# A gated linear attention layer whose chunk loop is written out: scores of the next chunk before the head sums, no GpSimd copies, output projection in two halves

## The reference, cut to what matters

```python
def gla_chunked(q, k, v, gk):
    # S_t = diag(exp(gk_t)) S_{t-1} + k_t v_t^T ; o_t = q_t S_t, per head
    def step(state, inp):
        qi, ki, vi, gi = inp
        b = jnp.cumsum(gi, axis=2)
        o_inter = jnp.einsum('bhcd,bhde->bhce', qi * jnp.exp(b), state)
        ...
        o_intra = jnp.einsum('bhij,bhje->bhie', att, vi)
        state = state * jnp.exp(b_last)[:, :, 0, :, None] + jnp.einsum('bhcd,bhce->bhde', ki * jnp.exp(b_last - b), vi)
        return state, o_inter + o_intra

def odd_mixer(h, w_in, gate_up, gate_b, onorm, w_out):
    p = h @ w_in                      # q, k, v, gate input gd, output gate og
    gk = jax.nn.log_sigmoid((gd @ gate_up + gate_b).astype(jnp.float32)) / GLA_GATE_NORM
    o = gla_chunked(q, k, v, gk)
    o = rmsnorm(o, onorm).reshape(B, S, VW) * jax.nn.silu(og)
    return o.astype(h.dtype) @ w_out
```

## Time and profile before

| what | value |
|---|---|
| median of 3 runs | 2069.48 us (2065.72 to 2070.42) |
| profiled execution: its own time | 2070.38 us |
| its span, first to last instruction | 2068.6 us |
| mean granted TensorE clock, share of full speed | 0.958 |
| TensorE busy | 1937.5 us, 94% of the span |
| VectorE, ScalarE, GpSimd busy | 620.2, 460.2 and 209.8 us |
| from chunk 0's first value matmul to the output projection's first matmul | 1312.82 to 1358.38 us |
| the output projection to its last residual add's end | 1358.38 to 1416.67 us |

### The profile page before, as it was taken

One profiled execution on the slowest core, in us unless ns is written; L12 is line 12 of the kernel. 1 busy time (PEld: TensorE's weight loads), 2 busy tenths in 40 slices (PEclk: granted clock), 3 DMA queues, 4 the chain that ended last, 5 costly groups with the idle time before them and its releaser, 6 DMA issues.

```text
span 2068.6 us, 22048 instructions
## 1 busy us (share of the span) xinstructions
PE 1937.5 (94%) x8209; PEld 960.4 (46%) x8209; DVE 620.2 (30%) x1029; ACT 460.2 (22%) x791; POOL 209.8 (10%) x238
## 2 busy tenths in 40 slices
PE   7999898999978999999998999989968999999997
PEld 3554888746453333333333443644453333333333
DVE  2153766532241232223123004211241222123223
ACT  3254332132311111111112004511311111111113
POOL 2000444110001000000000000220100000000000
PEclk9999998999968999999999999999968999999999
DMA  6210100025028999999995113104038999999992
GB/s 174 81 41 0 42 1 1 1 85 220 3 103 332 424 423 424 423 423 424 422 424 196 42 42 120 41 0 163 3 122 344 422 423 424 422 424 422 424 423 84
DMA packets 88654, 466.25 MB, mean 225 GB/s; under 512 B 22426, under 2 KB 24586, under 8 KB 47642
## 3 DMA queue, kind: packets, MB, share of 16 engines
q1 hardware_dynamic: 77024, 448.88, 53.5%
q10 hardware_dynamic: 6682, 8.25, 1.2%
q0 software_dynamic: 4896, 8.40, 1.1%
HBM read 468.64 MB, written 6.29 MB: 230 GB/s over the span
## 4 chain that ended last, share of the span: by engine, by line
PE 85%; DMA 6%; DVE 5%; ACT 2%; issue 1%; POOL 1%; SPq 0%; ACTq 0%; DVEq 0%; POOLq 0%
PE ps L987 80%; DMA W<-in_moe_w 5%; PE ps L1540 1%; PE ps L1511 1%; PE ps L1171 1%; DVE XI L1804 1%; DVE HT L1629 1%; DMA xin<-in_x 0%; PE ps L1483 0%; DVE XJ L1800 0%; DMA xg<-hrows,idc 0%; PE ps L1108 0%; ACT L690 0%; PE ps L1372 0%; POOL memN L573 0%
## 5 line engine op out<-in xcount | busy, mean ns | idle before, releaser
L987 PE MATMUL ps<-W,xgT 128*64 128x512 f32 x2048 | 457.4, 599 | 5.8 <-DMA W<-in_moe_w 3.0
L987 PE MATMUL ps<-HT,W 128*128 128x512 f32 (+1 forms) x896 | 405.4, 611 | 18.8 <-DVE HT L1629 10.4
L987 PEld LDWEIGHTS ps<-HT,W 128*128 128x128 f32 (+1 forms) x896 | 172.7, 195 | 239.2 <-issue 226.0
L987 PEld LDWEIGHTS ps<-W,xgT 128*64 128x64 f32 x2048 | 144.5, 138 | 289.8 <-issue 278.3
L2027 DVE TENSOR_TENSOR XT<-ps,XT 128x512 f32<-128x512 f32 x240 | 166.0, 692 | 236.9 <-PE ps L987 236.9
L987 PE MATMUL ps<-W,act 128*64 128x512 f32 x1024 | 232.3, 595 | 2.8 <-ACT ysb L950 2.8
L987 PE MATMUL ps<-spread,ysb 128*128 128x512 f32 x512 | 228.3, 599 | 3.2 <-ACT ysb L950 3.2
L2019 DVE TENSOR_TENSOR act<-ps,sl 128x256 f32<-128x256 f32 x64 | 26.9, 420 | 450.6 <-ACT sl L945 450.6
L987 PEld LDWEIGHTS ps<-spread,ysb 128*128 128x128 f32 x512 | 94.6, 190 | 136.5 <-issue 136.5
L941 ACT ACTIVATE hs<-ps 128x512 f32<-128x512 f32 x64 | 38.2, 597 | 438.9 <-PE ps L987 438.9
L987 PEld LDWEIGHTS ps<-W,act 128*64 128x64 f32 x1024 | 70.8, 137 | 136.4 <-issue 136.4
(11 more groups left out here) (361 smaller groups left out, 1781.6 us busy)
## 6 DMA issues: line engine op xcount, KB each, us to landing
W<-in_moe_w SPq DMA_DIRECT2D x256, 1024.0 KB, 17.0
W<-in_moe_w SPq DMA_DIRECT2D x64, 2048.0 KB, 16.2
W<-in_od_w_in SPq DMA_DIRECT2D x6, 2048.0 KB, 8.1
W<-in_ev_w_in SPq DMA_DIRECT2D x3, 2048.0 KB, 7.8
W<-in_xa_wq SPq DMA_DIRECT2D x2, 2048.0 KB, 8.6
W<-in_xa_wo SPq DMA_DIRECT2D x2, 2048.0 KB, 10.4
hrows<-hk ACTq DMA_DIRECT2D x8, 512.0 KB, 2.7
W<-in_od_w_out SPq DMA_DIRECT2D x2, 2048.0 KB, 7.8
```

The lines of the kernel that those rows point to most:

```text
L987: return te.matmul(o, l, r, start=first, stop=last)
```

## The change

The loops over the four chunks become straight code on TensorE, VectorE and ScalarE. Within it:
- GpSimd's copies and the tiles `gkc` and `gvc` are gone; TensorE reads `gk` and `gv` in place.
- A function `open_chunk(c)` holds the 4 transposes (bank 7) and the 4 score matmuls (bank 6) of a chunk. That of chunk 0 stands before the last gate projection; that of chunk c+1 stands behind chunk c's state matmuls and before its head sums. The last chunk has no transposes and no state matmuls.
- The head sums go to bank 0 and wait only for the squares. The copy of y out of banks 2 and 3 is waited for before the next chunk's values.
- ScalarE copies the turned keys of the next chunk after its copy of y and before the Ln. VectorE masks chunk 0 before the last gate multiply, and later chunks after the state's two operations. GpSimd's second multiply waits for all eight `og` tiles by a semaphore of its own, `og_in`.
- The output projection goes in two halves of 256 tokens, each 8 tiles of 8 matmuls with 256 columns. The first (banks 2 and 3, columns 0 to 255) waits for two chunks of `g_out` and for the last copy of y; the second (banks 0 and 1, columns 256 to 511) for all of `g_out`. VectorE adds both, in 16 adds.

The core of the diff:

```diff
@@ GpSimd, odd() @@
-                copy(0)
-                copy(1)
                 for c in range(NCH):
...
+                    pool.wait_ge(s["og_in"], KD)
                     g.tensor_tensor(y, y, og[:, :, c * CH:c * CH + CH], ALU.mult).then_inc(s["g_out"], 1)
-                    if c + 2 < NCH:
-                        copy(c + 2)
@@ ScalarE, odd() @@
+                def take_keys(c):
+                    act.wait_ge(s["g_turned"], c + 1)
+                    sc.activation(gkt[:, :], ps[:, 7, :], ACT.Copy).then_inc(s["g_tok"], 1)
+
                 for j in range(KD):
                     take(og[:, j, :], func=ACT.Silu)
+                    if j == KD - 2:
+                        take_keys(0)
...
-                with act.Fori(0, NCH) as c:
-                    act.wait_ge(s["g_turned"], c + 1)
-                    sc.activation(gkt[:, :], ps[:, 0, :], ACT.Copy).then_inc(s["g_tok"], 1)
+                for c in range(NCH):
                     act.wait_ge(s["g_y"], c + 1)
...
+                    if c + 2 < NCH:
+                        take_keys(c + 1)
                     act.wait_ge(s["g_sum"], c + 1)
-                    act.wait_ge(s["g_out"], c + 1)
-                    inverse_root(grs[:, :, :].rearrange("p h t -> p (h t)"), ps[:, 6, :], 256, 0, s["g_ln"], c + 1).then_inc(s["g_rs"], 1)
+                    if c:
+                        act.wait_ge(s["g_half"], c)
+                    inverse_root(grs[:, :, :].rearrange("p h t -> p (h t)"), ps[:, 0, :], 256, 0, s["g_ln"], c + 1).then_inc(s["g_rs"], 1)
@@ TensorE, odd() @@
+                def open_chunk(c):
+                    t = slice(c * CH, c * CH + CH)
+                    if c + 1 < NCH:
+                        for h in range(4):
+                            ins = te.transpose(ps[:, 7, h * P:h * P + P], gk[:, h, t], ident[:, :])
+                        ins.then_inc(s["g_turned"], 1)
+                    for h in range(4):
+                        ins = mm(ps[:, 6, h * P:h * P + P], gk[:, h, t], gq[:, h, t])
+                    ins.then_inc(s["g_mat"], 1)
+
                 for name in ("od_og0", "od_og1"):
                     slot = weights(name)
                     for j in range(4):
+                        if name == "od_og1" and j == 3:
+                            pe.wait_ge(s["g_scaled"], 1)
+                            open_chunk(0)
                         project(bank(), [(W8[slot][:, k, P * j:P * j + P], HT[:, k, :]) for k in range(KD)])
                 pe.wait_ge(s["proj_taken"], n["proj"])
...
+                for c in range(NCH):
+                    t = slice(c * CH, c * CH + CH)
+                    pe.wait_ge(s["g_masked"], c + 1)
+                    pe.wait_ge(s["g_state"], c + 1)
+                    if c:
+                        pe.wait_ge(s["g_sq"], 2 * c)
+                    for e in range(KD):
+                        o = ps[:, 2 + e // 4, P * (e % 4):P * (e % 4) + P]
+                        mm(o, gv[:, c, e * P:e * P + P], gat[:, e // 2, :], True, False)
+                        ins = mm(o, gsn[:, e // 2, P * (e % 2):P * (e % 2) + P], gq[:, e // 2, t], False, True)
+                    ins.then_inc(s["g_y"], 1)
+                    if c + 1 < NCH:
                         pe.wait_ge(s["g_tok"], c + 1)
                         for h in range(4):
-                            ins = mm(ps[:, 4 + h // 2, 256 * (h % 2):256 * (h % 2) + 256], gkt[:, h * P:h * P + P], gvc[b][:, 256 * h:256 * h + 256])
+                            ins = mm(ps[:, 4 + h // 2, 256 * (h % 2):256 * (h % 2) + 256], gkt[:, h * P:h * P + P], gv[:, c, 256 * h:256 * h + 256])
                         ins.then_inc(s["g_added"], 1)
-                        pe.wait_ge(s["g_sq"], c * 2 + 2)
...
+                        open_chunk(c + 1)
+                    pe.wait_ge(s["g_sq"], 2 * c + 1)
+                    for h in range(4):
+                        for u in range(2):
+                            ins = mm(ps[:, 0, h * P:h * P + P], ones[:, :], gsq[:, 2 * h + u, :], u == 0, u == 1)
+                    ins.then_inc(s["g_sum"], 1)
...
+                pe.wait_ge(s["g_out"], NCH // 2)
+                pe.wait_ge(s["g_sq"], 2 * NCH)
+                for mt in range(KD):
+                    if mt >= 2:
+                        pe.wait_ge(s["half_in"], KD + mt - 1)
+                    for k, (l, r) in enumerate(tiles(slice(0, SEQ // 2))(mt)):
+                        ins = mm(ps[:, 2 + mt % 2, 0:SEQ // 2], l, r, k == 0, k == KD - 1)
+                    ins.then_inc(s["half_done"], 1)
+                pe.wait_ge(s["g_out"], NCH)
+                pe.wait_ge(s["g_tok"], NCH - 1)
+                residual(tiles(slice(SEQ // 2, SEQ)), KD, at=0, cols=slice(SEQ // 2, SEQ))
@@ VectorE, odd() @@
-                with dve.Fori(0, NCH) as c:
+                for c in range(NCH):
+                    if c:
+                        mask(c)
+                    if c + 1 < NCH:
+                        dve.wait_ge(s["g_added"], c + 1)
+                        st.then(ve.tensor_tensor(gsn[:, :, :], ps[:, 4:6, :].rearrange("p b (h v) -> p (b h) v", h=2), gsn[:, :, :], ALU.add))
+                        ve.tensor_tensor(gsn[:, :, :], gsn[:, :, :], bcast(gnext[:, :, c:c + 1], [P, 4, 256]), ALU.mult).then_inc(s["g_state"], 1)
+                for mt in range(KD):
+                    dve.wait_ge(s["half_done"], KD + mt + 1)
+                    cols = slice(0, SEQ // 2)
+                    ve.tensor_tensor(XT[:, mt, cols], ps[:, 2 + mt % 2, cols], XT[:, mt, cols], ALU.add).then_inc(s["half_in"], 1)
+                residual(at=0, cols=slice(SEQ // 2, SEQ))
```

More of the change, by code:

```diff
@@ L987, in mm @@
                 return te.matmul(o, l, r, start=first, stop=last)
-            for name, first in (("hh_done", 1), ("hh_half", 1), ("y_done", 1), ("xg_turned", 1), ("g_added", 2), ("added", 8)):
+            for name, first in (("hh_done", 1), ("hh_half", 1), ("y_done", 1), ("xg_turned", 1), ("added", 8)):
                 pe.sem_inc(s[name], first)
@@ L1033, in weights, with residual @@
                 return slot
-            def residual(tiles_of, count, ready=None, between=None):
+            def residual(tiles_of, count, ready=None, between=None, at=2, cols=slice(0, SEQ)):
                 for mt in range(KD):
@@ new lines, in odd, with tiles @@
+                    pe.wait_ge(s["g_sq"], 2 * c + 1)
[3 more added lines that the diff above has]
+                    ins.then_inc(s["g_sum"], 1)
+                slots = [weights("od_o0"), weights("od_o1")]
+                def tiles(cols):
+                    return lambda mt: [(W8[slots[mt // 4]][:, k, P * (mt % 4):P * (mt % 4) + P], HT[:, k, cols]) for k in range(KD)]
@@ L1629, in norm, with residual @@
                     ve.scalar_tensor_tensor(dst[:, k, :], src[:, k, :], col(gain, first + k), rs[:, 0:width], ALU.mult, ALU.mult).then_inc(s["h_ready"], 1)
-            def residual(between=None):
+            def residual(between=None, at=2, cols=slice(0, SEQ)):
                 for mt in range(KD):
@@ L1635, in residual @@
                     dve.wait_ge(s["res_done"], n["res"] + mt + 1)
-                    ve.tensor_tensor(XT[:, mt, :], ps[:, 2 + mt % 2, :], XT[:, mt, :], ALU.add).then_inc(s["xt_ready"], 1)
+                    ve.tensor_tensor(XT[:, mt, cols], ps[:, at + mt % 2, cols], XT[:, mt, cols], ALU.add).then_inc(s["xt_ready"], 1)
                 n["res"] += 8
@@ L1895, in odd @@
                 dve.wait_ge(s["g_state"], 1)
-                with dve.Fori(0, NCH) as c:
-                    st.enter(c, 1)
-                    dve.wait_ge(s["g_mat"], c + 1)
-                    ve.tensor_tensor(gat[:, :, :], ps[:, 1, :].rearrange("p (h t) -> p h t", h=4),
-                                     bcast(tri[:, 1, :].unsqueeze(1), [P, 4, CH]), ALU.mult).then_inc(s["g_masked"], 1)
-                    dve.wait_ge(s["g_added"], c + 3)
-                    st.then(ve.tensor_tensor(gsn[:, :, :], ps[:, 4:6, :].rearrange("p b (h v) -> p (b h) v", h=2), gsn[:, :, :], ALU.add))
-                    ve.tensor_tensor(gsn[:, :, :], gsn[:, :, :], bcast(gnext[:, :, bass.ds(c, 1)], [P, 4, 256]), ALU.mult).then_inc(s["g_state"], 1)
-                    st.leave(NCH)
```

42 lines of the change are left out of this document (10 added, 32 removed).

## The result

The changed kernel took 2049.84 us (median; 2046.7 to 2050.52), the kernel before 2068.92 in the same comparison: ratio 0.9907 (0.989 to 0.9924; the numbers in brackets behind a ratio are its 95% interval). That is 19.1 us, where the prediction said about 14 to 15 and a range that ended at 2051. The profiled execution has a span of 2048.7 us against 2068.6, at a mean granted clock of 0.962 against 0.958.

A forecast was written before the change was run, and what follows sets the result against it. It took TensorE as the bound (85% of the chain), with time lost to its waits and half clock. Savings 1.07 + 3.04 + 8.67 − 0.32 + 2.47 + 0.27 = 15.2 us off 2070.4 gave 2055 us; range 2051 to 2060.5.

The forecast's parts named there:

- Before chunk 0: Ahead of the chunk loop: transposes and scores move before the last gate projection, so values start earlier; 1.07 us saved.
- Chunk periods: Start of one chunk's values to the next's: three periods take 27.05 us instead of 30.09; 3.04 us saved.
- Copies: GpSimd's copies in the chunks lie beside TensorE work and gated nothing after the first chunk; removing them is worth 0.
- ScalarE's queue: In the chunks: the key copy now stands before the Ln, with or without a third table load; cost 0.
- Behind chunk 3: After the last chunk: the projection's first half starts right behind the head sums, not after GpSimd; 8.67 us saved.
- The halves: Output projection in sixteen tiles: 0.32 us lost on steps, 2.47 saved from half clock, 0.27 saved at the last add.
- rival 1: At the projection's start TensorE still drops to the lower clock once: price 2.5 us, 2057.5 us; chance 0.09.
- (3): Rival: the projection's first half can't start early because some wait isn't satisfied: gain 5 us, 2065 us; chance 0.04.
- (4): Rival: weight loads bound the projection's halves, rows staying above 0.216 us; up to 55 us slower, 2109 us; chance 0.02.
- (2): Rival: in the chunks GpSimd holds VectorE every time, or is itself late: price up to 4.1 us, 2058 us; chance 0.07.
- The bound for chunks held in full: Worst case of the chunk loop: GpSimd holds VectorE's multiply fully each time, three periods 31.2 us, a loss of 1.2.
- the rest of the program shifted by 15: Code behind the odd layer: expected in the profile after to start some 15 us earlier, its own length unchanged.

The follow-up runs named there:

- fill_before: Kernel before plus four extra matmuls of 512 constant columns in three norms (both cross-attentions', the odd layer's), results unused: 2066.45 us, ratio 1.0002.
- b_shift: Kernel before plus one extra matmul of 384 constant columns in the middle of the odd layer's output projection, result unused: 2065.06 us, ratio 0.9987.

## Why the prediction was off
Inside the layer the mechanism was the one forecast; the total was too small. By its own steps:
- *Before chunk 0, 1.07 saved.* Measured 1.19: from the take to the first value 0.65 plus 1.33, for 3.17.
- *Chunk periods, 3.04 saved (8.85, 9.3, 8.9).* Measured 3.31 (8.82, 9.15, 8.81). VectorE sets the period with the mask behind its two state operations, and GpSimd held the multiply once, by 0.41, in chunk 1, as said.
- *Copies, worth 0; ScalarE's queue, 0.* The trace shows no wait for either. The key copy waited 0.23 us for its transposes, and only two table loads a chunk are left.
- *Behind chunk 3, 8.67 saved.* Measured 8.64 (6.83 us from the values to the projection, for 15.47).
- *The halves.* −0.32, 2.47 and 0.27. Measured together 2.14 + 0.27: start of the projection to the last add 55.46 for 57.60, and the Ln 2.50 behind that add for 2.77. The steps are 3.453 us, as the memory keys' were.
- *Rivals.* The clock at the start of the projection was 1.00 (rival 1 out), the first half started at once (3), rows of 256 columns cost 0.216 (4), GpSimd held VectorE for 0.41 once and for 0.06 once more (2).

These sum to 15.55 for 15.2. (The bound for chunks held in full is a loss of 1.1, not 1.2; nothing rests on it.) **The step that failed is "the rest of the program shifted by 15"**: the sum has no term for the code behind the layer, which puts its change at nothing. I had taken the clock as a cost only where the change removes a wait (2.47). The low end, 2051, had room for a shorter half clock behind the next norm, and none for anything later. Measured behind the layer were 2.6 us in the cross-attention and 1.3 in the experts, 3.9 in all, in code that the change doesn't touch.

Shown is what the 2.6 us are: TensorE's rows of the same matmuls at half clock, in two stretches of 6.8 and 3.4 us in before and one of 3.4 in the changed kernel. They vanish with the norm's wait filled, and differ with 0.6 or 2.2 us of extra work ahead. The second stretch also went in fill_before, where nothing was filled near it. For the experts' 1.3 us the profiles show which arrangement of the half clock goes with which length; no run sets the arrangement on purpose. That the 15.5 us by which the layer is shorter brought both about is argued from this. The expected gain in the layer was there, and the surplus can't be counted on: other edits ahead of it gave 81.6, 83.1 or 84.9 us in the cross-attention.

## What to carry to other kernels
When a part is written out by hand, take each engine's start and end from the timeline and add them up in the new order; that sum held here within 0.4 us in 15. But here waits of a few us on TensorE made the clock behind the edit hard to foretell: give the range several us for it, compare over many executions, as one kernel's lay up to 12 us apart (2058.3 to 2070.3), and read the layer's own stretch in the trace before you credit the edit with the rest. Where the wait can't be removed, a few matmuls into an unused bank kept the clock here, provided that TensorE really waits there; check that first, since the same four cost 3.4 us where it didn't.

## What the runs showed of the hardware that I had not expected
- Executions of one kernel go with its mean granted clock: before took 2058.3 to 2062.0 us at 0.965 and 2069.0 to 2070.7 at 0.958. Between kernels it is no measure: at 0.960 b_shift took 2065.05 to 2065.49 and before 2066.9 to 2068.6. Extra work can make a kernel faster: 0.64 us of it gave 3.1. The Trainium skill, page TensorE: Matmul & The Clock Gate, Part 1, says that the chip looks at activity on a clock of its own, which doesn't restart with the kernel, so that the number of slow matmuls differs from run to run. The traces agree: two profiles of before have 63.05 and 61.45 us for the same stretch of gate projections, with 6.8 and 3.4 us at half clock in it. Yet in the cross-attention behind the odd layer the pattern repeated in all three profiles of each kernel (85.8 to 86.0 and 83.3 us), and other kernels had 81.6, 83.1 and 84.9 for the same code.
- Behind the odd layer's norm, a wait of 3.60 us, the granted clock fell to the lower of its two levels, 1.2 GHz, in all twelve profiles without extra matmuls there; behind the same wait before the second cross-attention in nine of twelve. In four profiles it also fell later in that cross-attention, at the end of a wait of 1.60 us. Through the written-out chunks' waits of 0.3 to 1.1 us it stayed at 1.00, the 2.4 GHz level.
- VectorE's instruction with two SBUF inputs, started 0.55 us before GpSimd's running one ended, took 0.41 longer (1.63 for 1.22); the one that reads PSUM took 1.23 beside GpSimd.
